# Running a one-expert team and a two-expert team through the stages in turn, in a mixture-of-experts layer on one Trainium2 core

## What is computed

```python
def swiglu(h, wg, wu, wd):
    return (jax.nn.silu(h @ wg) * (h @ wu)) @ wd

logits = (xf @ router_w).astype(jnp.float32) + router_b.astype(jnp.float32)
top_logit, top_e = lax.top_k(logits, TOP_K)            # 2 of 8 for each of 256 tokens
top_w = jax.nn.softmax(top_logit, axis=-1)
...
y[rows of e] = swiglu(xf[rows of e], wg[e], wu[e], wd[e])   # wg, wu 1024 x 3584; wd 3584 x 1024
out = zeros.at[row_tok].add(y * row_w[:, None])
x = x + g2 * out
```

## Time and profile before

| | |
|---|---|
| median of 3 runs | 1650.5 us (1647.33 to 1651.12) |
| profiled execution, its own time | 1654.32 us |
| its span in the trace | 1652.4 us |
| TensorE busy | 1501.3 us (91%) |
| VectorE, ScalarE busy | 452.4 us (27%), 186.9 us (11%) |
| moved by DMA | 481.59 MB, mean 291 GB/s |

### The profile page before, as it was taken

The page is one execution under the profiler, slowest core; times in us unless marked ns, Lnnn a source line. Parts: engine busy times, 40 slices in busy tenths (PEclk is TensorE's granted clock), DMA queues, the critical chain, the costliest instruction groups (busy, mean ns, idle before and its releaser), DMA issues.

```text
span 1652.4 us, 16712 instructions
## 1 busy us (share of the span) xinstructions
PE 1501.3 (91%) x6912; PEld 739.5 (45%) x6912; DVE 452.4 (27%) x908; ACT 186.9 (11%) x401; POOL 2.5 (0%) x23
## 2 busy tenths in 40 slices
PE   5999989999998999867888899999887999998887
PEld 2566745555544767542223344533232444432332
DVE  5487734444442744340000011001100111010001
ACT  2123221000012232210000000000000001000000
POOL 0000000000000000000000000000000000000000
PEclk9999899999998999969999999999999999999998
DMA  9935625878862300059999999789999997899995
GB/s 346 350 105 203 218 94 182 274 269 295 313 241 89 104 1 1 0 234 409 418 412 408 418 414 346 289 322 414 412 413 411 413 410 270 297 393 418 416 407 229
DMA packets 151358, 481.59 MB, mean 291 GB/s; under 512 B 15816, under 2 KB 33608, under 8 KB 144112
## 3 DMA queue, kind: packets, MB, share of 16 engines
q1 hardware_dynamic: 149832, 478.64, 75.5%
q10 hardware_dynamic: 1448, 1.84, 0.4%
HBM read 479.41 MB, written 1.06 MB: 291 GB/s over the span
## 4 chain that ended last, share of the span: by engine, by line
PE 72%; DMA 21%; SPq 2%; DVE 2%; issue 1%; ACT 1%; DVEq 0%; ACTq 0%
PE bank L1433 23%; DMA ring<-in_moe_wu 10%; PE bank L1305 9%; PE bank L1466 9%; DMA ring<-in_moe_wg 8%; PE bank L1075 7%; PE bank L1323 5%; PE bank L1066 4%; PE bank L1282 3%; SPq L734 2%; DMA ring<-in_ada_w 1%; DMA ring<-in_moe_wd 1%; PE bank L1202 1%; PE bank L1056 1%; PE bank L1152 1%
## 5 line engine op out<-in xcount | busy, mean ns | idle before, releaser
L1433 PE MATMUL bank<-ring,h_T 128*32 128x512 f32 (+1 forms) x2240 | 323.0, 640 | 56.5 <-DMA ring<-in_moe_wg 30.6
L1466 PE MATMUL bank<-ring,m_qk_T 128*32 128x512 f32 (+2 forms) x1344 | 259.6, 626 | 33.5 <-issue 29.5
L1433 PEld LDWEIGHTS bank<-ring,h_T 128*32 128x32 f32 (+1 forms) x2240 | 102.6, 122 | 263.4 <-issue 260.4
L1433 PE MATMUL bank<-ring,cmp_region 128*128 128x512 f32 x448 | 196.3, 593 | 0.0
L1466 PEld LDWEIGHTS bank<-ring,m_qk_T 128*32 128x32 f32 (+2 forms) x1344 | 95.6, 133 | 192.8 <-issue 192.5
L1305 PE MATMUL bank<-ring,h_T 128*128 128x384 f32 (+1 forms) x448 | 158.3, 507 | 2.1 <-ACT h_T L797 1.3
L1433 PEld LDWEIGHTS bank<-ring,cmp_region 128*128 128x128 f32 x448 | 84.1, 190 | 103.8 <-issue 103.8
L1075 PE MATMUL bank<-ring,h_T 128*128 128x512 f32 (+1 forms) x320 | 117.6, 517 | 0.0
L1305 PEld LDWEIGHTS bank<-ring,h_T 128*128 128x128 f32 x448 | 84.2, 192 | 64.0 <-issue 16.8
L2116 DVE SCALAR_TENSOR_TENSOR m_s_region<-s_v,bank 128x512 f32<-128x512 f32 x20 | 13.7, 687 | 329.7 <-ACT s_v L967 329.7
L956 ACT ACTIVATE m_qk_T<-bank 128x512 f32<-128x512 f32 x35 | 20.9, 597 | 641.7 <-PE bank L1449 641.2
(11 more groups left out here) (320 smaller groups left out, 1016.2 us busy)
## 6 DMA issues: line engine op xcount, KB each, us to landing
ring<-in_moe_wg SPq DMA_DIRECT2D x56, 2048.0 KB, 21.3
ring<-in_moe_wu SPq DMA_DIRECT2D x56, 2048.0 KB, 21.8
ring<-in_moe_wd SPq DMA_DIRECT2D x56, 2048.0 KB, 21.2
ring<-in_ada_w SPq DMA_DIRECT2D x28, 1024.0 KB, 8.8
ring<-in_ada_w SPq DMA_DIRECT2D x10, 2048.0 KB, 14.2
ring<-in_w_in SPq DMA_DIRECT2D x10, 2048.0 KB, 10.7
ring<-in_ffn_wg SPq DMA_DIRECT2D x6, 1536.0 KB, 10.3
ring<-in_ffn_wu SPq DMA_DIRECT2D x6, 1536.0 KB, 9.0
```

The costliest lines, as they stand in the source:

```text
L1433: last = mm(b[c0:c1, :], xT[st.team % 2][:, k, c0:c1], w, start=k == 0, stop=k == KC - 1)
L1466: last = mm(ps[half][c0:c1, :], hbT[:, unit, 128 * q + c0:128 * q + c1], down_at(slot, 512)[:, q, 512 * half:512 * half + 512], start=st.b ...
```

## The change

The teams are renumbered (single 0, pair 1, single 2, pair 3, pair 4), with the same token capacities by rank. Teams 0 and 1 now go through the four spans in turn: stage 0 of team 0, stage 0 of team 1, stage 1 of team 0, and so on; then teams 2 and 3 in the same way; then team 4 alone. Since another team's down product comes between two stages of a team, PSUM banks 0 and 1 can't hold the sum any more: a run (the stages in which `begin` to `end` lie without a change of team) is one stage for teams 0 to 3, and DVE copies its result into one of two SBUF areas `ysum`, or adds to it (`run_out`). The areas and the turned one-hot matrices of the second two teams lie in `bias`, which the attention of the layers used before. Token gathers of team 1 are done ahead of the first stage, through banks 0 and 1; the other gathers, turns and scatters get new places in tables.

```diff
-TEAMS = (((0, 0, 96), (1, 96, 128)), ((2, 0, 128),), ((3, 0, 96), (4, 96, 128)), ((5, 0, 128),), ((6, 0, 64), (7, 64, 128)))
-SLOT_RANK, SLOT_CAP = (2, 7, 0, 3, 6, 1, 4, 5), (96, 32, 128, 96, 32, 128, 64, 64)
+TEAMS = (((0, 0, 128),), ((1, 0, 96), (2, 96, 128)), ((3, 0, 128),), ((4, 0, 96), (5, 96, 128)), ((6, 0, 64), (7, 64, 128)))
+SLOT_RANK, SLOT_CAP = (0, 2, 7, 1, 3, 6, 4, 5), (128, 96, 32, 128, 96, 32, 64, 64)
...
 STAGES = []
-for _t in range(len(TEAMS)):
+for _teams in ((0, 1), (2, 3), (4,)):
     for _s in range(len(SPANS)):
-        STAGES.append(Stage(_t, _s, sum(st.units for st in STAGES)))
+        for _t in _teams:
+            STAGES.append(Stage(_t, _s, sum(st.units for st in STAGES)))
+for _j, _st in enumerate(STAGES):
+    _st.begin = _j == 0 or STAGES[_j - 1].team != _st.team
+    _st.end = _j == len(STAGES) - 1 or STAGES[_j + 1].team != _st.team
+    _st.run = sum(b.end for b in STAGES[:_j])
...
+GATHER_A, GATHER_B = {2: (6, 2), 3: (8, 0), 4: (14, 2)}, {2: (7, 1), 3: (8, 2), 4: (15, 1)}
+RETURN_IN = {9: 0, 10: 1, 17: 2, 18: 3}
+PICKED_IN, WEIGHED_IN, TURNED_IN = {5: (2, 3), 13: (4,)}, {11: (2, 3), 13: (4,)}, {1: (0, 1), 11: (2, 3), 13: (4,)}
...
+        ysum = [ysb, bias_flat[:, 0:1024]]
...
             gather(moe, range(4), BLK, 1, banks=(7,))
             gather(moe, range(4, 8), BLK, banks=(2,))
+            gather(moe, range(4), BLK, 2, banks=(0,), q=1)
+            gather(moe, range(4, 8), BLK, banks=(1,), q=1)
...
             def moe_down(j):
 
                 st = STAGES[j]
-                if st.begin and st.team:
-                    pe.wait_ge(moe["y_0"], st.team)
-                    pe.wait_ge(moe["y_1"], st.team)
+                if st.begin and st.run:
+                    pe.wait_ge(moe["y_taken"], 2 * st.run)
...
-            def team_out(team):
-
-                dve.wait_ge(moe["d"], team + 1)
-                y_out(moe, 0, do)
-                down_done(dve, STAGES[len(SPANS) * team + len(SPANS) - 1], 0)
-                y_out(moe, 1, do)
+            def run_out(st):
+
+                for half in range(2):
+                    c = slice(512 * half, 512 * half + 512)
+                    y = ysum[st.team % 2][:, c]
+                    if half:
+                        down_done(dve, st, st.units - 1)
+                    else:
+                        dve.wait_ge(moe["d"], st.run + 1)
+                    if st.first:
+                        do(V.tensor_copy(y, ps[half][:, :]), moe["y_taken"])
+                        continue
+                    whole = st.team == len(TEAMS) - 1
+                    if not whole:
+                        do(TTop(y, ps[half][:, :], y, ALU.add), moe["y_taken"])
+                    if st.last:
+                        do(TTop(y, ps[half][:, :] if whole else y, gate[:, 1, c], ALU.mult), moe["y_1" if half else "y_0"])
...
-                if s == 0 and team:
-                    team_out(team - 1)
...
+                if j and STAGES[j - 1].end:
+                    run_out(STAGES[j - 1])
-            team_out(len(TEAMS) - 1)
+            run_out(STAGES[-1])
```

More of the change, by code:

```diff
@@ L310, in __init__ @@
         self.f0, self.units = SPANS[s]
-        self.begin, self.end = s == 0, s == len(SPANS) - 1
+        self.first, self.last = s == 0, s == len(SPANS) - 1
         self.members = range(len(TEAMS[team]))
@@ L947, in _ @@
             gathered_in(moe, range(4), BLK, 1, do, bank=7)
+            gathered_in(moe, range(4), BLK, 3, do, into=1, bank=0)
             def turned_in(j, unit):
@@ L976, in _ @@
                     turned_in(j - 1, 1)
[L977 to L980, removed]
+                for team, (at, _) in GATHER_A.items():
+                    if at == j:
+                        gathered_in(moe, range(4), BLK, 2 * team + 1, do, into=team % 2, bank=7)
             act.wait_ge(over_ready, 1)
@@ L1472, in moe_down, with moe_scatter @@
                             last.then_inc(moe["d"], 1)
-            def moe_scatter(team, n, bank=7, added=True):
+            def moe_scatter(team, n, bank=7):
                 half, tt = divmod(n, 2)
@@ new lines, in beside @@
+                if at == 0 and j in TURNED_IN:
+                    teams = TURNED_IN[j]
+                    if teams == (2, 3):
+                        pe.wait_ge(moe["added"], 8)
+                    elif teams == (4,):
+                        pe.wait_ge(moe["turn_evac"], 2)
+                    turn_picks(moe, (0, 1) if len(teams) == 2 else (1,), {0: 3, 2: 5, 4: 6}[teams[0]])
+                for team in range(2, len(TEAMS)):
+                    if GATHER_A[team] == (j, at):
+                        if team != 3:
+                            pe.wait_ge(moe["turn_evac"], 1 if team == 2 else 3)
+                        gather(moe, range(4), BLK, {2: 4, 3: 4, 4: 6}[team], banks=(7,), q=int(team == 3))
+                    if GATHER_B[team] == (j, at):
+                        pe.wait_ge(moe["in_act"], team + 1)
+                        gather(moe, range(4, 8), BLK, banks=(7,), q=int(team == 3))
@@ L2093, in _ @@
             gathered_in(moe, range(4, KC), BLK, 2, do, bank=2)
+            gathered_in(moe, range(4, KC), BLK, 4, do, into=1, bank=1)
             do(TTop(over_rank, rank[:, :, 0:N_EXP], over_first(slot_cap, TT), ALU.subtract))
@@ L2127, in _ @@
             for j, st in enumerate(STAGES):
[L2128 to L2138 removed]
+                returned = RETURN_IN.get(j)
@@ L2139, in _ @@
+                if returned is not None:
+                    add_team(returned, 0)
+                for team in PICKED_IN.get(j, ()):
+                    onehot(team, team == 3)
+                for team in WEIGHED_IN.get(j, ()):
+                    onehot_weighted(team, team > 2, 0 if team == 2 else 1)
+                if j in TURNED_IN:
+                    n = TURNED_IN[j][0] // 2
+                    picks_turned(moe, n + 1, do, pickT_area[n % 2][:, 0:256 * len(TURNED_IN[j])])
                 for unit in range(st.units):
@@ L2140, in _ @@
                     gated(j, unit)
-                if s == 1 and team:
-                    add_team(team - 1, 1)
-                if s == 3 and following:
-                    gathered_in(moe, range(4, KC), BLK, 2 * following + 2, do, into=following % 2, bank=7)
+                if returned is not None:
+                    add_team(returned, 1)
+                for team, (at, hook) in GATHER_B.items():
+                    if (at, hook) == (j, 1):
+                        gathered_in(moe, range(4, KC), BLK, 2 * team + 2, do, into=team % 2, bank=7)
@@ L2145, in _ @@
                 for unit in range(st.units):
                     multiplied(j, unit)
-                if s == 0 and team:
-                    team_out(team - 1)
-                if s == 1 and team:
-                    add_team(team - 1, 2)
-                    add_team(team - 1, 3)
-            team_out(len(TEAMS) - 1)
+                for team, (at, hook) in GATHER_B.items():
+                    if (at, hook) == (j, 2):
+                        gathered_in(moe, range(4, KC), BLK, 2 * team + 2, do, into=team % 2, bank=7)
```

92 lines of the change are left out of this document (38 added, 54 removed).

## The result

The changed kernel takes 1596.81 us in the median of 4 runs (1594.3 to 1602.14), beside 1650.38 us for the kernel before: ratio 0.9683, 95% interval 0.9656 to 0.971. The profiled execution took 1597.0 us, its span 1595.1 us. The prediction said 1597 us.

The account below looks back on a forecast made before the run. The weight stream was taken to bound the whole expert phase: 853.9 + 3.8 for its ends + 3 for the ring = 860.7 us from 718.35, plus 19.7, span 1598.8; + 1.9 - 3.8 gives 1597 us, range 1587 to 1615.

Parts of the forecast that it names:

- The two bounds that take turns: Expert phase before: weight stream full in pair teams, TensorE full in single teams, where DMA falls to 275 GB/s.
- The size of the stream: Expert weights: 168 loads, 352.3 MB at 412.6 GB/s, take 853.9 us if never starved of slots.
- TensorE's 620 us: Teams 0 to 3: TensorE's whole work at full clock, 620 us, against 640 us of stream.
- The margin of 20 us in 640: Teams 0 to 3: the stream needs 20 us more than TensorE, so it bounds the whole phase.
- The ring: Seven weight slots bridge the uneven blocks, 13.4 us of issued loads left in the widest gap; cost 3 us.
- Rival A: Seven weight slots are too few in the seven single blocks: 40 us lost, 1637 us; chance 0.13.
- Rival B: TensorE at its lower clock becomes the bound in teams 0 to 3: 1641 us; chance 0.06, slower than before 0.02.
- Two arguments: Against many slow pieces: idle leaves room for about one a cycle of twelve, and a late TensorE doesn't idle.
- The added DVE work: `run_out` for 17 runs instead of 5: 32 more DVE instructions, 22 us in the phase, hidden; cost nothing.
- The start and the last part: Team 1's gather ahead of the first stage costs nothing; 19.7 us lie behind the last landing.
- The sum: Whole kernel: span 1598.8 us, plus 1.9 for the execution, less 3.8 for the median, gives 1597 us.

Follow-up runs that it names:

- run 3: Kernel before with half of the gate and up matmuls left out, all loads kept: 1595.52 us, ratio 0.9669.
- run 1: Kernel before with only the changed kernel's numbering of teams, teams still one after the other: 1650.38 us, ratio 1.0003.
- run 7: Changed kernel with every transpose of the hidden block made three times, same result: 1605.8 us.
- run 8: Changed kernel with every transpose of the hidden block made six times, same result: 1630.1 us.
- Run 9: Changed kernel in which DVE copies each half of banks 0 and 1 eight times more before taking it: 1612.16 us.
- run 2: Changed kernel with the single and pair team of each two swapped, the pair's stage first: 1597.99 us, ratio 0.9679.
- run 4: Changed kernel with half of the gate and up matmuls left out, all loads kept: 1598.28 us, ratio 0.968.

## Why the prediction was right

**The two bounds that take turns.** Shown by runs 3 and 1: relieve TensorE and the valleys fill; keep the teams in blocks and they stay, wherever the single teams stand.

**The size of the stream.** 853.9 us of transfer, 3.8 for its ends and 3 for the ring were predicted, 860.7 us; it took 861.5. The parts hold too: 858.9 us with TensorE far from the bound (857.7 predicted), 2.6 us for what the ring and TensorE still cost (3 predicted for the ring). The rate of 412 GB/s in 740 to 1340 us is the rate of the pair teams before (412.6).

**TensorE's 620 us.** From 726.95 to 1362.86 us lie 635.9 us, less 20.4 of waits up to 1359 us and 0.47 ahead of team 4: 615.0 us. The last down piece of team 3 and the transposes before it, which the 620 us count, come later, inside team 4's first stage (7.07 and about 0.7 us, at 1403.51 and 1369.88 us). Together 622.8 us, of which 3.4 are two slow pieces: 619 at full clock against 620 predicted. The margin of 20 us in 640 agrees with the 21 us of waits. Of the rates at which it would be used up, run 7 shows a third passed on (9 of 27 us), run 8 half (33 of 68).

**The ring.** By arithmetic 2.6 loads stay in flight with seven slots, 1.6 with six, fewer than one with five. Measured cost: 2.6 at most, 7.4 on top of it and 40.6 on top of it. Rival A named the right mechanism; it did not come with seven slots.

**The clock.** Rival B did not come. Of the 84 pieces in teams 0 to 3 two took 8.77 us (at 780.70 and 1285.61 us), and the clock of the stretch is 0.99. Two arguments were given. One was that slow pieces stand behind idle of 2.35 and 3.16 us, with room for about one a cycle. That did not hold as stated: behind 2.21 and 4.31 us of waits a piece took 8.77 us, but behind 2.70, 3.11 and 3.17 us it took 7.07. So that only two pieces were slow is in part luck. The other was that an engine that is late has no idle time; in run 8, where TensorE never waits for weights in teams 0 to 3, the clock was 1.00 in the stretches read (860 to 900 and 1140 to 1180 us), and no piece of teams 0 to 3 took 8.77 us. TensorE is busy for 1465.7 us in the changed kernel, before for 1501.3, with the same 6912 matmuls, because most slow pieces are gone; they had stood in stretches where the stream was full, so this is no part of the gain.

**The added DVE work.** Cost nothing at its real size: two instructions of 0.69 us a run (four in the last run of each of teams 0 to 3), no wait for `y_taken`. DVE is busy for 474.4 us instead of 452.4, the 22 us that were added up. The reasoning named only the product of the next stage as what is queued behind `run_out`. Run 9 showed that the picks of the next teams and the last handover of the program are nearer; the step was right by its margin and incomplete in its list.

**The start and the last part.** The gather of team 1 ahead of the first stage cost nothing (10.1 us from the first gather to the first piece against 10.6 before). Predicted were 13, with both gathers at 6.42 us each; together they took 10.24 us, and the second one lies largely under the evacuation of the first, which I had not named. The remaining difference in the spans, 1598.8 predicted and 1595.1 measured, is + 0.8 for the stream, - 1.3 for the last piece at full clock and - 3.1 for the start. The last is not the change: the first expert load is issued between 714.5 and 716.3 us in some profiled executions of these kernels and between 718.3 and 719.3 in others, in kernels whose code ahead of it is the same (719.22 in run 2, 719.08 in run 4, 715.46 in run 7), as it is at 714.53 and 716.05 us in runs 1 and 3, which keep the old stages. The sum then took off 3.8 us, because the median of the kernel before lay that far below its profiled execution. In the changed kernel it lies 0.2 us below (1597.0 and 1596.81 us). The 3.7 us by which the span was forecast too long and the 3.6 us taken off without a counterpart cancel: that the median agrees to 0.2 us is luck.

## What to carry to other kernels

When two resources are each full in turn, add up each one's need over the whole phase before anything else; if the larger sum is well below the phase, work of the two kinds can be interleaved, and the time goes to that sum. Then check that the buffer bridges the longest stretch in which the other resource falls behind, in units of transfers still in flight: here the last of seven slots was worth 7.4 us and the last two together 40.6. Whether a longer ring would have bridged the blocks of the old order was not run; by the figures above a single team takes TensorE 147.6 us and its 21 loads 107 us, so an estimate is 41 us, or eight slots more. Where a result is handed over more often, list everything that queues behind the handing instruction, the end of the program too.

## What the runs showed of the hardware

A wait of TensorE of 2.5 to 3.2 us did not by itself send the next piece to the low clock. In the pair team before, every second piece of the earlier trace rows took 8.77 us, behind 2.35 and 3.16 us of idle. In the changed kernel a piece behind 3.11 us (871.39 us) ran in 7.07, and so did four in a row in team 4, with waits as long and TensorE busy for 78% of the time. Timeline of TensorE in team 4 of the changed kernel:

```profile
1373.10 7.09 PE L1449 MATMUL bank<-ring,h_T 128*64 128x512 f32 x32 [2.47 <-DMA ring<-in_moe_wg]
1383.34 7.09 PE L1449 MATMUL bank<-ring,h_T 128*64 128x512 f32 x32 [3.15 <-DMA ring<-in_moe_wu]
1393.57 7.09 PE L1449 MATMUL bank<-ring,h_T 128*64 128x512 f32 x32 [3.14 <-DMA ring<-in_moe_wu]
1403.51 7.07 PE L1481 MATMUL bank<-ring,m_qk_T 128*32 128x512 f32 x64 [2.86 <-DMA ring<-in_moe_wd]
```

The Trainium skill, TensorE: Matmul & The Clock Gate, "HAM oscillation — how this bites in real kernels", describes a kernel in which a wait for data ahead of each tile, of about 3 to 5 us, made every next tile start at the low clock. The trace of the kernel before shows this at every second piece of the earlier trace rows (8.77 against 7.07 us), the stretch above at none of four, at waits of 2.47 to 3.15 us. What makes the difference stays open. Where the stream is the bound the slow pieces cost nothing: the stretches with them ran at 402 to 417 GB/s.
